# A two-layer hybrid diffusion block on one core: scratch cleared by POOL, the convolution's mean moved, and fillers and norm steps reordered on TensorE

## The chip, the cores and the metric

The kernel runs on one core of a Trainium2 chip. The metric is the device time of one execution in microseconds (us). Engines are called PE (TensorE), DVE (VectorE), ACT (ScalarE), POOL (GpSimd) and SP (SyncE, which issues the DMAs).

## The reference

256 context tokens and 256 latent tokens of width 1024 go through two layers. Cut to what matters here:

```python
for l in range(DEPTH):                      # DEPTH = 2
    mod_x, mod_c = silu(c) @ w_mod[l] + b_mod[l], silu(c_ctx) @ w_mod[l] + b_mod[l]   # 6 x 1024 each
    hx = modulate(rmsnorm(x, g_norm1[l]), mod_x[0], mod_x[1])      # hc likewise from the context
    px = split_cols(hx @ w_in[l])
    m = mlstm_mixer(...)       # matrix memory, 4 heads, both directions; then a layer norm per head
    d = diff_attention(...)    # softmax(q1 k1) - lam * softmax(q2 k2), 4 heads
    c = conv_mixer(...)        # 31 taps, then layernorm over 256 channels, then silu
    x = x + mod_x[2] * (concatenate([m, d, c]) @ w_out[l])
    h = modulate(rmsnorm(x, g_norm2[l]), mod_x[3], mod_x[4])
    x = x + mod_x[5] * (swiglu(h) if l == 0 else top_2_of_8_experts(h))
return rmsnorm(x, g_final)
```

The inputs and outputs are float32.

## The kernel before, in words

Each engine runs one hand-written program, and the order of its code is the order of its instructions; semaphores tie the engines together. Activations lie feature-major (128 features by 512 tokens, KD = 8 tiles). A weight comes in 1 MB chunks through a ring of four slots, loaded by SP: the load of chunk n waits until PE has used chunk n - 4. A product in float32 is made of three passes (`product`, L535): a leading part and a rest of both factors. The leading part is a copy, on DVE (`leading_bits`, L1539, L1540) or on ACT (`lead`, L1217) with the rest on DVE (`split_rest`, L1554).

PE is kept from idling before some waits by fillers: `spin(o, n)` (L542) issues n matmuls of ones, 128x256, whose result nobody reads. The profile shows two instructions for each float32 matmul, so n fillers are 2n rows. The tables `SPIN` and `SPIN_FIRST` hold the counts.

The places that the change touches, in the order of time:

- **Opening.** PE makes eight modulation chunks (`modulation_chunk`, L557) as they land, each followed by `SPIN_FIRST[i]` fillers. After chunk `NORM_AFTER` stands `norm(0, 0)`: column sums of squares, eight matmuls of 128x1 (L596) that wait for ACT's squares and DVE's sums. One chunk later stands `norm_spread` (L607), which spreads 1/rms over the partitions. ACT takes the root in `deviation` (L1107) and copies the modulation rows in `modulation_rows` (L1134). `turn_modulation` (L584) turns the rows into columns. After the last one DVE, ACT, DVE make the first tile of h, and the first projection starts.
- **Gate rows.** `gate_rows` on DVE clears a 64x3072 piece of the scratch (L1572), and then splits the second and third weight chunk of the projection.
- **Start of attention**, once a layer. PE: the last head's sums (`memory_sums`, L716), scores(0) (L752), the convolution's mean (`conv_mean`, L814), modulation chunks, its variance (`conv_variance`, L823, which waits for ACT's squares L1310), fillers, the transposes of the heads (L741), `conv_spread` (L830), scores(1), fillers, then the attention steps. DVE: `memory_sums`, `conv_centre` (L1844), `memory_moments`, `maxima` (L1769), and so on. ACT: a modulation row (L1134), a table load, the convolution's squares.
- **The other norms.** `norm(l, which)` on PE: fillers `SPIN["squares", ...]`, sums of squares, then `modulation(1, ...)`, which puts `norm_spread` behind its first chunk (the argument `between`).
- **Router and experts.** PE: the second norm of layer 1 as above, the logits (L914), transposes (L922), eight fillers, ranks (L930 to L934), `SPIN["moe"]` fillers, the gather of the first expert's tokens (L956), then the expert loop (L989, L1009), eight trips here.

The lines that set the norm's order before:

```python
for i in batch(l, first):
    modulation_chunk(l, first, i)
    if i == first and turned and turned[0] not in MOD_ENDS:
        turn_modulation(*turned[0])
    if i == first and between:
        between()
```

## Time and profile before

| | |
|---|---|
| median of three runs | 1466.93 us (1465.52 to 1468.47) |
| the profiled execution's own time | 1464.65 us |
| its span | 1462.9 us |
| mean granted PE clock over the span | 0.973 of full speed |
| PE busy | 1395.8 us (95%) |
| DVE / ACT / POOL busy | 982.7 / 632.6 / 181.1 us |
| HBM read | 265 MB, 182 GB/s over the span |

The span runs from the first to the last instruction; the rest of the execution's time lies around it. A busy PE includes the fillers. The granted clock is given per stretch; 1.00 is 2.4 GHz and 0.50 is 1.2 GHz.

### The profile page before, as it was taken

Reading aid. Unit: us, or ns where it says so; the run is one execution under the profiler, and the core shown is the slowest. Engines: PE = TensorE matmul, PEld = TensorE weight load, DVE = VectorE, ACT = ScalarE, POOL = GpSimd, SP = SyncE. Lnnn points to the kernel's source line nnn. Section 1 sums busy time; section 2 is a strip of 40 time slices with the busy share of each in tenths; the row PEclk is TensorE's granted clock in tenths of the full one; section 3 lists DMA queues with packets and bytes.
Section 4 is the critical chain, followed back from the end, with each engine's and each line's share of the span. In section 5 each row is a group of like instructions: output and inputs, shape, how many; then the busy total and the mean of one; then the engine's idle time right before and its main releaser. Section 6 shows DMA issues by size and latency. Waiting matters only on the chain.

```text
span 1462.9 us, 20612 instructions
## 1 busy us (share of the span) xinstructions
PE 1395.8 (95%) x7756; PEld 1144.4 (78%) x7756; DVE 982.7 (67%) x1476; ACT 632.6 (43%) x997; POOL 181.1 (12%) x134
## 2 busy tenths in 40 slices
PE   7999999989999999999999999898999999999996
PEld 4778787567688888888869887687888888888885
DVE  3755876755744344354469685656898998998896
ACT  3434334652310110010035434635677777777774
POOL 0039970000000000000003960000000000000000
PEclk8999999989999999999999999998999999999998
DMA  9254443322323222222233223149977977977940
GB/s 396 103 201 173 173 173 115 124 108 87 144 91 110 87 103 99 79 109 89 112 116 144 87 87 116 58 150 426 380 289 310 346 305 302 356 291 307 355 171 29
DMA packets 30881, 267.07 MB, mean 183 GB/s; under 512 B 3424, under 2 KB 3552, under 8 KB 4960
## 3 DMA queue, kind: packets, MB, share of 16 engines
q1 hardware_dynamic: 30816, 266.16, 47.7%
q8 instruction: 46, 0.75, 0.2%
q14 instruction: 19, 0.16, 0.0%
HBM read 265.09 MB, written 1.05 MB: 182 GB/s over the span
## 4 chain that ended last, share of the span: by engine, by line
PE 84%; DVE 8%; issue 3%; ACT 3%; DMA 2%; SPq 0%; DVEq 0%; ACTq 0%
PE ps L535 38%; PE ps L989 17%; PE ps L1009 7%; PE ps L852 3%; PE ps L557 3%; PE ps L716 2%; PE ps L752 1%; PE ps L681 1%; PE ps L771 1%; PE ps L542 1%; DMA sb_arena<-mod 1%; DVE sb_egu_lo L2007 1%; PE ps L584 1%; DVE sb_h_lo L1540 1%; PE ps L762 1%
## 5 line engine op out<-in xcount | busy, mean ns | idle before, releaser
L535 PE MATMUL ps<-sb_h_hi,sb_w_hi 128*128 128x512 f32 (+1 forms) x640 | 241.9, 378 | 3.0 <-DVE sb_w_lo L1540 2.7
L535 PE MATMUL ps<-sb_h_hi,sb_w_lo 128*128 128x512 f32 (+1 forms) x640 | 239.5, 374 | 0.0
L535 PE MATMUL ps<-sb_h_lo,sb_w_hi 128*128 128x512 f32 (+1 forms) x640 | 239.4, 374 | 0.0
L989 PE MATMUL ps<-sb_egu_lo,sb_h_lo 128*128 128x512 f32 (+1 forms) x384 | 145.2, 378 | 0.0
L535 PEld LDWEIGHTS ps<-sb_h_hi,sb_w_hi 128*128 128x128 f32 x640 | 121.1, 189 | 28.9 <-DVE sb_w_lo L1540 3.6
L535 PEld LDWEIGHTS ps<-sb_h_hi,sb_w_lo 128*128 128x128 f32 x640 | 121.0, 189 | 21.5
L535 PEld LDWEIGHTS ps<-sb_h_lo,sb_w_hi 128*128 128x128 f32 x640 | 121.2, 189 | 20.7
L1539 DVE CAST sb_w_hi<-sb_arena 128x2048 fp32r<-128x2048 f32 (+1 forms) x38 | 45.5, 1197 | 126.0 <-PE ps L535 114.7
L2007 DVE TENSOR_TENSOR sb_egu_lo<-sb_arena,sb_con_r 128x1024 fp32r<-128x1024 f32 x98 | 115.2, 1216 | 15.3 <-ACT sb_con_r L1360 15.1
L2018 DVE TENSOR_TENSOR sb_ew_lo<-sb_arena,sb_ew_hi 128x1024 fp32r<-128x1024 f32 x88 | 107.1, 1216 | 11.5 <-ACT sb_ew_hi L1373 11.5
L2152 POOL TENSOR_SCALAR sb_arena<-sb_arena,sb_small 128x512 f32<-128x512 f32 (+1 forms) x60 | 104.8, 1746 | 5.9
L1373 ACT ACTIVATE sb_ew_hi<-sb_arena 128x1024 fp32r<-128x1024 f32 x88 | 91.7, 1052 | 30.5 <-PE ps L1009 30.5
L1333 ACT ACTIVATE sb_arena<-ps 128x512 f32<-128x512 f32 x22 | 13.2, 599 | 202.1 <-PE ps L535 202.0
L2007 DVE TENSOR_TENSOR sb_egu_lo<-sb_arena,sb_x_r 128x1024 fp32r<-128x1024 f32 x82 | 96.4, 1216 | 0.5
L1360 ACT ACTIVATE sb_con_r<-sb_arena 128x1024 fp32r<-128x1024 f32 x96 | 95.9, 1051 | 0.0
L1554 DVE TENSOR_TENSOR sb_w_lo<-sb_arena,sb_w_hi 128x2048 fp32r<-128x2048 f32 x24 | 57.4, 2394 | 53.6 <-ACT sb_w_hi L1217 53.4
L989 PE MATMUL ps<-sb_con_r,sb_h_lo 128*128 128x512 f32 (+1 forms) x224 | 83.1, 371 | 3.4 <-DVE sb_egu_lo L2007 3.4
L1540 DVE TENSOR_TENSOR sb_w_lo<-sb_arena,sb_w_hi 128x2048 fp32r<-128x2048 f32 (+1 forms) x38 | 85.0, 2236 | 1.3
L989 PEld LDWEIGHTS ps<-sb_egu_lo,sb_h_lo 128*128 128x128 f32 x384 | 73.4, 191 | 13.4
L989 PE MATMUL ps<-sb_con_r,sb_hs_lo 128*128 128x512 f32 (+1 forms) x224 | 82.4, 368 | 0.0
L1360 ACT ACTIVATE sb_x_r<-sb_arena 128x1024 fp32r<-128x1024 f32 x80 | 80.4, 1059 | 0.0
L2138 POOL MEMSET sb_arena<- 128x60 f32 x2 | 0.6, 301 | 600.1 <-ACT sb_H L1119 600.1
(325 smaller groups left out, 3037.2 us busy)
## 6 DMA issues: line engine op xcount, KB each, us to landing
sb_arena<-experts SPq DMA_DIRECT2D x90, 1536.0 KB, 8.8
sb_arena<-mod SPq DMA_DIRECT2D x48, 1024.0 KB, 4.9
sb_arena<-in SPq DMA_DIRECT2D x24, 1024.0 KB, 4.8
sb_arena<-gate SPq DMA_DIRECT2D x11, 1024.0 KB, 4.8
sb_arena<-up SPq DMA_DIRECT2D x11, 1024.0 KB, 4.7
sb_arena<-out SPq DMA_DIRECT2D x8, 1024.0 KB, 6.1
sb_arena<-down SPq DMA_DIRECT2D x8, 1024.0 KB, 4.8
sb_arena<-down SPq DMA_DIRECT2D x4, 768.0 KB, 4.1
```

What stands on the lines that cost most here:

```text
L535: ins = pe.matmul(o, left[a], right[b], start=(k == first and n == 0), stop=(k == final and n == len(PRODUCTS) - 1))
L557: ins = pe.matmul(o[g * TILE:(g + 1) * TILE, 0:CHUNK], cond[:, k, at:at + TILE], w[:, k, :], start=(i == first and q == 0), stop=(i == bat ...
L989: ins = pe.matmul(o, x[:, k, :], w[:, span, :], start=(k == 0 and n == 0), stop=(k == KD - 1 and n == 2))
L1009: ins = pe.matmul(ps[:, m, :], left[a], right[b][:, m * 512:(m + 1) * 512], start=(f == 0 and n == 0), stop=(f == ET - 1 and n == len(PROD ...
L1360: f(glead[x % 4], experts[:, t, a * HALF:(a + 1) * HALF].rearrange("p (a n) -> p a n", a=4), ACT.Copy)\
L1373: f(ew_hi[:, t % 2, :], experts[:, t, 2 * HALF:], ACT.Copy).then_inc(down_leading, 1)
L1539: settled(v.tensor_copy(hi, x), ("hi", key))
L1540: v.tensor_tensor(lo, x, hi.bitcast(F32), ALU.subtract).then_inc(*dve_done.tick(key))
L1554: v.tensor_tensor(w_lo[:, n % RING], chunk_view(chunk), w_hi[:, c % SPLIT].bitcast(F32), ALU.subtract)\
L2007: v.tensor_tensor(egu_lo[t][:, a * HALF:(a + 1) * HALF].rearrange("p (a n) -> p a n", a=4), experts[:, t, a * HALF:(a + 1) * HALF].rearran ...
L2018: v.tensor_tensor(ew_lo[t][:, :], experts[:, t, 2 * HALF:], ew_hi[:, t % 2, :].bitcast(F32), ALU.subtract).then_inc(down_split, 1)
L2152: g.tensor_scalar(p, u, w[:, j:j + 1], None, ALU.mult).then_inc(*pool_done.tick(("product", l, j)))
```

## The change

DVE no longer clears the scratch; POOL does, ahead of its four small memsets, and DVE waits for it ahead of the gate arithmetic. `conv_mean` moves on PE from behind scores(0) to ahead of it, and `conv_centre` on DVE from behind the last head's sums to ahead of them. `norm_spread` now follows the sums of squares at once, with three fillers ahead of its wait (none in the opening), and the modulation chunks follow it. In the opening the norm moves one chunk ahead, ACT's root goes ahead of the first modulation row, and fillers are redistributed. Filler counts: squares (1, 0) 2 to 7, six and five new ones ahead of the convolution's variance, moe 5 to 12.

```diff
-NORM_AFTER = 3
+NORM_AFTER = 2
...
-SPIN = {("squares", 0, 0): 0, ("squares", 0, 1): 2, ("squares", 1, 0): 2, ("squares", 1, 1): 0,
+SPIN = {("squares", 0, 0): 0, ("squares", 0, 1): 2, ("squares", 1, 0): 7, ("squares", 1, 1): 0,
...
-        "router": 8, "moe": 5}
+        ("variance", 0): 6, ("variance", 1): 5, "spread": 3, "router": 8, "moe": 12}
...
-SPIN_FIRST = (8, 1, 1, 0, 1, 5, 2, 0)
+SPIN_FIRST = (8, 2, 0, 2, 1, 4, 2, 0)
...
-            def modulation(l, first, between=None):
+            def modulation(l, first):
...
-                    if i == first and between:
-                        between()
...
-                    modulation(1, MOD_NORM[l, which], lambda: norm_spread(l, which))
+                    norm_spread(l, which)
+                    modulation(1, MOD_NORM[l, which])
...
             def norm_spread(l, which):
                 lo = low(l) if which else 0
+                o = open_bank(("nscale", l, which))
+                if l + which:
+                    spin(o, SPIN["spread"])
                 pe.wait_ge(*dve_done.at(("ndiag", l, which)))
-                o = open_bank(("nscale", l, which))
...
                 memory_sums(l, NH - 1, 1)
+                conv_mean(l)
...
                 scores(0)
-                conv_mean(l)
                 fill(l, 1)
...
             def conv_variance(l):
                 lo = low(l)
+                o = open_bank(("cvar", l))
+                spin(o, SPIN["variance", l])
                 pe.wait_ge(*act_done.at(("csq", l)))
-                o = open_bank(("cvar", l))
...
             squared(0, 0)
+            deviation(0, 0)
             modulation_rows(0, 0)
-            deviation(0, 0)
...
-                settled(v.memset(scratch[0:64, 2 * T:8 * T], 0.0), ("clear", l))
                 split(("in", l, IN_ORDER[1]))
                 split(("in", l, IN_ORDER[2]))
                 dve.wait_ge(*act_done.at(("gln", l)))
+                dve.wait_ge(*pool_done.at(("clear", l)))
...
+                conv_centre(l)
                 memory_sums(l, NH - 1, 1)
-                conv_centre(l)
...
                 pool.wait_ge(*act_done.at(("h", l, 0, KD - 1)))
+                g.memset(scratch[0:64, 2 * T:8 * T], 0.0).then_inc(*pool_done.tick(("clear", l)))
                 g.memset(upad[:, :, :, 0:PAD], 0.0)
```

PE in the opening, before (L557 is a modulation chunk, L542 fillers, L596 the sums of squares, L607 the spread, L584 a turn of modulation rows):

```order
L557 MATMUL ps<-sb_arena,sb_cond 32x256 x8
L542 MATMUL ps<-sb_con 128x256
L557 MATMUL ps<-sb_arena,sb_cond 32x256 x8
L596 MATMUL ps<-sb_con,sb_arena 128x1 x8
L557 MATMUL ps<-sb_arena,sb_cond 32x256 x8
L584 MATMUL ps<-sb_con,sb_tiny 128x4x2 x2
L542 MATMUL ps<-sb_con 128x256
L607 MATMUL ps<-sb_rstd,sb_con 128x512
L557 MATMUL ps<-sb_arena,sb_cond 32x256 x8
```

and the same place now (line numbers move a little: L594 is the sums, L608 the spread, L582 the turn):

```order
L557 MATMUL ps<-sb_arena,sb_cond 32x256 x8
L594 MATMUL ps<-sb_con,sb_arena 128x1 x8
L557 MATMUL ps<-sb_arena,sb_cond 32x256 x8
L542 MATMUL ps<-sb_con 128x256 x2
L608 MATMUL ps<-sb_rstd,sb_con 128x512
L557 MATMUL ps<-sb_arena,sb_cond 32x256 x8
L582 MATMUL ps<-sb_con,sb_tiny 128x4x2 x2
L542 MATMUL ps<-sb_con 128x256
L557 MATMUL ps<-sb_arena,sb_cond 32x256 x8
```

The sums stand ahead of the fourth chunk and the spread ahead of the fifth, each one chunk earlier.

PE at the first norm of layer 1, before (L535 is the first product of the projection):

```order
L542 MATMUL ps<-sb_con 128x256 x2
L596 MATMUL ps<-sb_con,sb_H 128x1 x8
L557 MATMUL ps<-sb_arena,sb_cond 32x256 x8
L584 MATMUL ps<-sb_con,sb_modrow_odd 128x3x2 x2
L607 MATMUL ps<-sb_rstd,sb_con 128x512
L557 MATMUL ps<-sb_arena,sb_cond 32x256 x16
L542 MATMUL ps<-sb_con 128x256 x4
L535 MATMUL ps<-sb_h_hi,sb_wg_hi 128x512
```

and now:

```order
L542 MATMUL ps<-sb_con 128x256 x7
L594 MATMUL ps<-sb_con,sb_H 128x1 x8
L542 MATMUL ps<-sb_con 128x256 x3
L608 MATMUL ps<-sb_rstd,sb_con 128x512
L557 MATMUL ps<-sb_arena,sb_cond 32x256 x8
L582 MATMUL ps<-sb_con,sb_modrow_odd 128x3x2 x2
L557 MATMUL ps<-sb_arena,sb_cond 32x256 x16
L542 MATMUL ps<-sb_con 128x256 x4
```

Three fillers have taken the place of a chunk and a turn ahead of the spread, and the chunk and the turn stand behind it.

PE at the start of attention in layer 0, before (L716 the last sums, L752 scores, L814 the mean, L823 the variance):

```order
L716 MATMUL ps<-sb_arena 128x96 x20
L752 MATMUL ps<-sb_arena 128x256 x2
L814 MATMUL ps<-sb_arena,sb_con 128x512 x2
L557 MATMUL ps<-sb_arena,sb_cond 32x256 x16
L823 MATMUL ps<-sb_con,sb_kq 128x1 x8
```

and now (L718 the sums, L815 the mean, L754 scores, L825 the variance):

```order
L718 MATMUL ps<-sb_arena 128x96 x20
L815 MATMUL ps<-sb_arena,sb_con 128x512 x2
L754 MATMUL ps<-sb_arena 128x256 x2
L557 MATMUL ps<-sb_arena,sb_cond 32x256 x16
L542 MATMUL ps<-sb_con 128x256 x6
L825 MATMUL ps<-sb_con,sb_kq 128x1 x8
```

The mean and the scores have changed places, and six fillers stand ahead of the variance.

## Rows read from the trace of the kernel before

**Rows 1.** The page's first part: busy time, share of the span, instructions.
```profile
PE 1395.8 (95%) x7756; PEld 1144.4 (78%) x7756; DVE 982.7 (67%) x1476; ACT 632.6 (43%) x997; POOL 181.1 (12%) x134
```
**Rows 2.** Windows: stretch, length, busy of PE, PEld, DVE, ACT, POOL, clock, DMA, GB/s.
```profile
23.20:33.40 10.20, 10.20 (x53) 5.91 (x53) 3.18 (x6) 2.17 (x2) 0.00 (x0) 0.50 1.02 421
...
255.30:262.10 6.80, 6.03 (x17) 3.23 (x16) 4.86 (x12) 3.29 (x10) 0.00 (x0) 0.50 0.11 43
...
746.80:753.60 6.80, 6.80 (x46) 2.98 (x42) 3.14 (x6) 1.68 (x5) 0.00 (x0) 0.50 0.39 154
903.80:910.60 6.80, 5.68 (x17) 4.90 (x18) 1.61 (x6) 4.24 (x10) 0.00 (x0) 0.50 0.58 225
976.50:993.30 16.80, 16.72 (x147) 13.90 (x146) 8.06 (x40) 8.40 (x20) 0.00 (x0) 0.90 0.68 269
```
**Rows 3.** Timeline of PE, opening: start, length, instructions, idle time before and releaser.
```profile
21.49 1.07 PE L557 MATMUL ps<-sb_arena,sb_cond 128*32 128x256 f32 x16 [2.06 <-DMA sb_arena<-mod]
22.49 2.99 PE L596 MATMUL ps<-sb_con,sb_arena 128*128 128x1 f32 x16
...
29.14 1.91 PE L607 MATMUL ps<-sb_rstd,sb_con 128*128 128x512 f32 x2
...
37.52 1.07 PE L557 MATMUL ps<-sb_arena,sb_cond 128*32 128x256 f32 x16
39.10 0.61 PE L584 MATMUL ps<-sb_con,sb_modrow_odd 128*128 128x8 f32 x4 [0.50 <-ACT sb_modrow_odd L1134]
```
**Rows 4.** Timeline of PE: sums of squares, and five fillers twice.
```profile
744.75 1.92 PE L596 MATMUL ps<-sb_con,sb_H 128*128 128x1 f32 x16 [2.43 <-ACT sb_H L1100]
...
906.65 4.37 PE L542 MATMUL ps<-sb_con 128*128 128x256 f32 x10
...
993.34 2.40 PE L542 MATMUL ps<-sb_con 128*128 128x256 f32 x10
```
**Rows 5.** Timeline of ACT, the first projection chunk's leading part.
```profile
30.13 1.91 ACT L1217 ACTIVATE sb_w_hi<-sb_arena 128x2048 fp32r<-128x2048 f32 x1 [4.35 <-DMA sb_arena<-in]
```
**Rows 6.** Timeline of DVE, the clear and the split behind it.
```profile
54.48 2.62 DVE L1572 MEMSET sb_arena<- 64x3072 f32 x1 [0.58 <-issue]
...
58.40 2.29 DVE L1540 TENSOR_TENSOR sb_w_lo<-sb_arena,sb_w_hi 128x2048 fp32r<-128x2048 f32 x1
```
**Rows 7.** Timeline of PE, the product that waits for that split.
```profile
60.74 0.50 PE L535 MATMUL ps<-sb_h_hi,sb_w_hi 128*128 128x512 f32 x1 [1.53 <-DVE sb_w_lo L1540]
```
**Rows 8.** Timeline of POOL, its first memset in layer 0.
```profile
50.88 0.30 POOL L2138 MEMSET sb_arena<- 128x60 f32 x1 [50.45 <-ACT sb_H L1119]
```
**Rows 9.** Timeline of PE, start of attention in layer 0.
```profile
253.16 1.95 PE L823 MATMUL ps<-sb_con,sb_kq 128*128 128x1 f32 x16 [2.96 <-ACT sb_kq L1310]
...
257.43 2.04 PE L830 MATMUL ps<-sb_rows_n,sb_con 128*128 128x512 f32 x2 [0.78 <-ACT sb_arena L1278]
...
260.56 3.16 PE L542 MATMUL ps<-sb_con 128*128 128x256 f32 x10
...
264.71 0.44 PE L762 MATMUL ps<-sb_con,sb_arena 128*128 128x128 f32 x2
```
**Rows 10.** Timeline of PE, second norm of layer 0.
```profile
374.28 1.67 PE L607 MATMUL ps<-sb_rstd,sb_con 128*128 128x512 f32 x2 [0.36 <-DVE sb_rstd L1524]
```
**Rows 11.** Timeline of PE, first norm of layer 1.
```profile
746.60 1.81 PE L557 MATMUL ps<-sb_arena,sb_cond 128*32 128x256 f32 x16
...
749.21 2.05 PE L607 MATMUL ps<-sb_rstd,sb_con 128*128 128x512 f32 x2
...
754.23 1.99 PE L542 MATMUL ps<-sb_con 128*128 128x256 f32 x8
```
**Rows 12.** Timeline of PE, the convolution's variance in layer 1.
```profile
904.92 1.87 PE L823 MATMUL ps<-sb_con,sb_kq 128*128 128x1 f32 x8 [2.54 <-ACT sb_kq L1310]
```
**Rows 13.** Timeline of PE, the gather.
```profile
996.86 3.84 PE L956 MATMUL ps<-sb_kq,sb_H 128*128 128x128 f32 x32 [1.11 <-DVE sb_kq L1977]
```
**Rows 14.** Timeline of ACT, its first work on the gathered tokens.
```profile
1000.74 1.08 ACT L1348 ACTIVATE sb_h_lo<-ps 128x512 fp32r<-128x512 f32 x2 [12.39 <-PE ps L956]
```

## The prediction

> **What bounds the kernel now.** I read the page's busy line first. PE works 1395.8 of 1462.9 us [rows 1], so a gain must come from PE's waits, from PE's clock, or from PE work that is not needed. The timeline shows PE without a gap through the projections, the dense layer and most of the expert loop; the change touches only the seams between them. So I read the seams next, in windows with their granted clock, and then PE's timeline there. In four seams the clock stood at 0.50, which is 1.2 GHz, for 10.2, 6.8, 6.8 and 6.8 us [rows 2]. Shortly before the first fall PE had waited 2.06 us [rows 3], before the others 2.4 to 3.0 (the rows come below), and each time sums of one column stood beside the wait (L596, L823); the reader is to see that the wait itself is short and the slow stretch behind it long. The fillers show what the clock is worth: ten rows (five fillers) take 2.40 us at 993.34 and 4.37 us at 906.65 [rows 4]. So a filler costs 0.48 us at full clock and up to 0.87 at half.
>
> **The change, part by part.** Gains are negative.
>
> *A, opening.* The sums of squares took 2.99 us behind chunk 3, mostly at half clock [rows 3]; at full clock sixteen such rows take 1.92 [rows 4]. They now stand in the 2.06 us wait ahead of chunk 3. PE then holds less work than the loads need time, so the last chunk's landing is the bound. The first projection chunk was there at 30.13 [rows 5], two modulation chunks follow it in SP's order, and a chunk of 1.05 MB at 421 GB/s [rows 2] takes 2.5 us: they land near 32.6 and 35.1. The last chunk began at 37.52 [rows 3], so at most 2.4 us are gained. A new wait of some 2 us ahead of chunk 6 can drop the clock again, which would leave 1.2. I take -1.9 (0 to -2.4). ACT's exchanged root and row copy cost nothing: the row is needed only for the turn, behind the spread.
>
> *B, the clear.* DVE's memset of 2.62 us plus 0.58 us ahead of it go [rows 6]; the split behind them ended at 60.69, and PE had waited 1.53 us for it [rows 7]. PE keeps its own pace up to there, so no more than the 1.53 can be gained. POOL starts at 50.88, when the last tile of h is done [rows 8], and its memset has no row in this trace: the bounds are 0.3 us (its small ones) and several us; DVE's 2.62 [rows 6] is the nearest row. DVE needs the cleared piece only behind two splits, over 7 us of its own work (twice 3.5 us), so the wait is hidden; the pads behind it on POOL are wanted only when the convolution's input is made, much later. In layer 1 nothing is gained, as PE did not wait there. I take -1.3 (0 to -1.5). The Trainium skill's page "SBUF — State Buffer", section "Who interferes with whom", says that a DVE copy or cast in a two-port mode and a POOL instruction block each other for their whole length. By it the memset would hold DVE's cast of the last tile of h for up to 2 us, and B would be -1.1; no row here shows a POOL memset of that length.
>
> *C, attention's start in layer 0.* Moving the mean alone gains nothing: ACT's squares wait for a modulation row and a table load, not for the centred rows, and DVE only changes the order of the same work. But six fillers (2.9 us) fill the 2.96 us wait [rows 9]. With the clock up, L830 takes about 1.0 instead of 2.04, the ten filler rows 2.4 instead of 3.16 [rows 4, 9] and the scores between them 0.5 less. The 0.78 us wait of L830 [rows 9] was for the bank that the first scores held; now the mean's older bank is next in turn, which is free. Together 3.0 us until the first turn at 264.71. DVE's chain to that turn runs through the same spread and the same scores, and gains less, since its own heads' work stands between. I take -2.4 (0 to -2.9).
>
> *D, second norm of layer 0.* The spread began at 374.28 behind one chunk (1.0 us), mostly waiting for DVE [rows 10]; three fillers take 1.44. It starts 0.1 us later, and gains up to 0.7 (1.67 to 0.97) if the clock holds. The first wait and the one-column sums ahead of it are unchanged, so I doubt that: -0.1 (-0.7 to +1.5, three fillers at half clock).
>
> *E, first norm of layer 1.* Seven fillers (3.4 us) end as ACT's squares are there; two left a wait of 2.43 [rows 4]. Chunk and turn (746.60 to 749.21) leave the way of the spread. Sums until 746.67, three fillers until 748.1, spread until 749.2 at full clock; then three chunks, the turn, four fillers: 749.2 + 2.8 + 0.5 + 1.95 = 754.5, against 755.87 before (behind the fillers from 754.23 [rows 11]). The projection starts 1.4 us earlier. DVE has its first tile ready by then, since it starts 2 us earlier too. I take -1.3 (0 to -1.4).
>
> *F, attention's start in layer 1.* Five fillers fill 2.54 us [rows 12]. The ten rows at 906.65 then take 2.40 instead of about 4.2 (they end at 910.85), and the sums ahead of them about 0.95 instead of 1.87 [rows 4, 12]. DVE's normalised heads are ready when those fillers begin. I take -2.4 (0 to -2.5).
>
> *G, router.* PE is busy for 16.72 of 16.80 us between the second norm's sums and the ranks [rows 2], so what is added there moves the ranks: three fillers, 1.44, less the short wait of the spread. +1.2 (0, if the clock comes better, to +1.5).
>
> *H, fillers ahead of the experts.* Seven more fillers last 3.4 us, and PE waited only 1.11 there before the gather [rows 13]. The gather starts 2.3 us late. Behind it ACT had been idle for 12.39 us [rows 14]; it converts the tokens and then works without a gap into the loop, so the loop starts late by as much. +2.3 (0 to +3.4, if the register load between also waits for the fillers).
>
> The sum is -9.4 + 3.5 = **-5.9 us**. The profiled execution took 1464.65, its span 1462.9, and the median of the runs is 1466.93. Against the profiled execution this gives 1458.75, and on the median's scale, which I forecast, **1461.0 us**.
>
> **The rivals.**
>
> *The clock is not held (0.21).* Fillers stop the idling, but the one-column sums stay, and at 374.28 the spread took 1.67 us, so the clock fell in it, with a wait of only 0.36 us next to those sums. For it: that row [rows 10]. Against it: in E and F the empty stretch shrinks by more than half. Then A gives -1.2, B -1.3, C only the bank's 1.0, and G and H cost 3.5: 0 in all, 1466.9 us.
>
> *The expert stage does not care (0.14).* Its weights load at the same time, and if the first tiles set its start, H and part of G are free. Against it: ACT's first conversion waited for the gather, not for a load [rows 14]. Without H the time is 1458.7.
>
> *Fillers outlast their waits (0.07), the slower side.* The three fillers ahead of each spread stand on the path, and where the clock is already half when they start, they take 2.5 us each time. It decides from the point where a norm's sums begin at half clock: +1.5 in D, +2.0 in E, +2.5 in G, with H's +2.3, less A, B and the bank in C (3.5): +4.8, 1471.7 us.
>
> The change not doing what it says is excluded by the order of instructions. POOL's clear taking as much from DVE as it frees is inside B.
>
> **How the numbers follow.** The forecast's own case has 0.58. A measurement of this kernel can tell about 0.2%, 2.9 us, from no change. The forecast and the second rival are faster by more: 0.72. The first rival is within it: 0.21. Slower: 0.07. The best of all bounds is -11.4, 1455.5; I end the range there, and at the other side at 1466.0, where the forecast's case with half of its clock gains and most of the first rival's neighbourhood lie.
>
> **What would show it.** Right: the clock at 1.00 around 255, 750 and 905 on the new time axis; the last modulation chunk of the opening near 35; no wait of PE for the second split; ten filler rows of about 2.4 us ahead of layer 1's head transposes; PE busy to the very start of the gather. Wrong, for the gains: windows at 0.50 at these places again. Wrong, for the costs: a gather as early behind the ranks as the 3.5 us of before, or an expert loop that starts as early after a later gather. Wrong as a whole, if PE waits inside the projections, where it never did.

## The result, and the profile after

The changed kernel takes **1455.86 us** (median of four executions, 1453.85 to 1456.15), the kernel before 1466.22 us beside it (1465.41 to 1468.47). The ratio is 0.9924, with a 95% interval of 0.9907 to 0.9941: 10 us faster, where 5.9 were forecast. The two profiled executions differ by 8.5 us in their spans. One execution of the kernel before, of 1982.8 us at a mean granted clock of 0.648, is in a slow state and is left out everywhere below.

The first part of the changed kernel's page, against [rows 1]:

```profile
PE 1396.8 (96%) x7822; PEld 1148.8 (79%) x7822; DVE 982.6 (68%) x1474; ACT 632.5 (43%) x997; POOL 186.6 (13%) x136
```

PE has 66 instructions more and hardly more busy time, in a span 8.5 us shorter. Windows of the changed kernel at the places of [rows 2], and two that are new (columns as there):

```profile
20.90:24.30 3.40, 3.40 (x20) 1.86 (x21) 0.45 (x1) 0.38 (x1) 0.00 (x0) 0.51 1.01 422
245.00:262.00 17.00, 16.46 (x114) 10.57 (x108) 14.02 (x35) 9.26 (x23) 0.00 (x0) 1.00 0.42 146
736.00:747.00 11.00, 10.49 (x89) 7.07 (x88) 6.77 (x13) 6.42 (x12) 0.00 (x0) 1.00 0.48 174
895.00:899.00 4.00, 3.82 (x23) 3.09 (x22) 1.62 (x6) 3.02 (x8) 0.00 (x0) 1.00 0.83 328
963.20:966.60 3.40, 3.40 (x12) 2.25 (x15) 0.66 (x3) 0.07 (x1) 0.00 (x0) 0.54 0.53 217
973.50:980.30 6.80, 6.80 (x32) 6.62 (x32) 4.29 (x26) 3.07 (x9) 0.00 (x0) 0.53 1.01 416
```

The clock is up (1.00, 2.4 GHz) at both starts of attention and at the first norm of layer 1, as forecast; the opening has 3.4 us near 1.2 GHz instead of 10.2. The last two lines are the other side: the router, which had one slow stretch before, has two. PE's timeline there, from the second norm's sums to the gather:

```profile
961.95 1.02 PE L594 MATMUL ps<-sb_con,sb_arena 128*128 128x1 f32 x8 [1.12 <-ACT sb_arena L1102]
962.84 2.86 PE L542 MATMUL ps<-sb_con 128*128 128x256 f32 x6
965.49 1.00 PE L608 MATMUL ps<-sb_rstd,sb_con 128*128 128x256 f32 x2
...
970.55 4.47 PE L916 MATMUL ps<-sb_small,sb_H 128*128 128x8 f32 x32
974.88 3.65 PE L924 MATMUL ps<-sb_con,sb_H 128*128 128x128 f32 x16
...
984.06 5.43 PE L542 MATMUL ps<-sb_con 128*128 128x256 f32 x24
989.32 3.73 PE L958 MATMUL ps<-sb_kq,sb_H 128*128 128x128 f32 x32
```

Three fillers take 2.86 us, double their price at full clock, and the twelve ahead of the gather fill the wait of [rows 13] and more. The last row has no wait: the gather now stands behind its fillers.

The seams read best as distances between two fixed instructions of PE, taken from each profile's timeline. Here they are for both profiles of the kernel before (the second is experiment e5) and three of the changed one (the first, e1, e16), in us:

| stretch of PE | before | before, e5 | changed | e1 | e16 |
|---|---|---|---|---|---|
| first chunk lands | 7.49 | 6.65 | 6.68 | 6.57 | 7.24 |
| A: from there to the first product | 35.11 | 33.46 | 32.71 | 32.86 | 32.17 |
| B: first product to the second split's product | 18.14 | 18.13 | 16.63 | 16.63 | 16.63 |
| to the end of the last head's sums, layer 0 | 184.97 | 184.93 | 184.94 | 184.83 | 188.71 |
| C: from their end to the first turn | 19.00 | 18.84 | 16.05 | 16.05 | 16.05 |
| D: fillers to projection, second norm, layer 0 | 11.38 | 11.37 | 12.17 | 12.18 | 12.04 |
| E: fillers to projection, first norm, layer 1 | 14.58 | 16.21 | 13.13 | 13.19 | 13.17 |
| F: last modulation chunk to the convolution's spread | 9.98 | 10.28 | 7.21 | 7.21 | 7.21 |
| to the second norm's sums, layer 1 | 64.19 | 63.77 | 62.72 | 63.76 | 62.75 |
| G: sums to logits | 6.00 | 6.00 | 8.60 | 8.55 | 8.60 |
| logits to ranks | 10.83 | 9.17 | 12.47 | 12.49 | 12.47 |
| H: ranks to gather | 4.55 | 4.55 | 6.30 | 6.30 | 6.29 |
| gather to the output's first matmul | 452.35 | 452.02 | 451.86 | 451.82 | 452.40 |
| span | 1462.9 | 1455.9 | 1454.4 | 1456.2 | 1458.0 |

Apart from the opening (A, 0.7 us), the touched stretches repeat within 0.15 us in these three profiles of the changed kernel. Kernels of the experiments whose code at C is the same are less regular: over fourteen profiles C took 16.05 us in eight, 16.7 to 16.8 in two and 17.3 in four, while F took 7.21 in every profile with its fillers. And the kernel before alone has spans of 1462.9 and 1455.9, and the changed one 1454.4 to 1458.0: one pair of profiles doesn't carry a difference of a few microseconds.

### The profile page after: what moved, and what is told of

Read it like the earlier page. It is cut to its first block, busy times and chain, and to the rows that moved or that the text cites. A ratio compares the mean times of both kernels' runs of the same rounds, so it can differ in the third digit from the quotient of the medians.

```text
span 1454.4 us, 20738 instructions
## 1 busy us (share of the span) xinstructions
PE 1396.8 (96%) x7822; PEld 1148.8 (79%) x7822; DVE 982.6 (68%) x1474; ACT 632.5 (43%) x997; POOL 186.6 (13%) x136
## 4 chain that ended last, share of the span: by engine, by line
PE 83%; DVE 7%; ACT 4%; issue 3%; DMA 3%; SPq 0%; DVEq 0%; ACTq 0%
PE ps L535 38%; PE ps L991 17%; PE ps L1011 7%; PE ps L854 4%; PE ps L557 3%; PE ps L718 2%; DMA sb_arena<-mod 2%; PE ps L542 2%; PE ps L683 1%; PE ps L754 1%; PE ps L773 1%; DMA sb_arena<-in 1%; DVE sb_egu_lo L2009 1%; DVE sb_ew_lo L2020 1%; PE ps L582 1%
## 5 line engine op out<-in xcount | busy, mean ns | idle before, releaser
L535 PE MATMUL ps<-sb_h_hi,sb_w_hi 128*128 128x512 f32 (+1 forms) x640 | 241.8, 378 | 1.5 <-DVE sb_w_lo L1542 1.1
L535 PE MATMUL ps<-sb_h_hi,sb_w_lo 128*128 128x512 f32 (+1 forms) x640 | 239.5, 374 | 0.0
L535 PE MATMUL ps<-sb_h_lo,sb_w_hi 128*128 128x512 f32 (+1 forms) x640 | 239.4, 374 | 0.0
L535 PEld LDWEIGHTS ps<-sb_h_hi,sb_w_hi 128*128 128x128 f32 x640 | 121.1, 189 | 27.2 <-DVE sb_w_lo L1542 2.0
L535 PEld LDWEIGHTS ps<-sb_h_hi,sb_w_lo 128*128 128x128 f32 x640 | 121.0, 189 | 21.6
L535 PEld LDWEIGHTS ps<-sb_h_lo,sb_w_hi 128*128 128x128 f32 x640 | 121.1, 189 | 20.6
L2020 DVE TENSOR_TENSOR sb_ew_lo<-sb_arena,sb_ew_hi 128x1024 fp32r<-128x1024 f32 x88 | 107.2, 1218 | 11.6 <-ACT sb_ew_hi L1375 11.6
L1335 ACT ACTIVATE sb_arena<-ps 128x512 f32<-128x512 f32 x22 | 13.2, 599 | 202.1 <-PE ps L535 202.0
L2140 POOL MEMSET sb_arena<- 64x3072 f32 x2 | 5.6, 2820 | 592.0 <-ACT sb_H L1121 592.0
```

What stands on the lines that cost most here:

```text
L535: ins = pe.matmul(o, left[a], right[b], start=(k == first and n == 0), stop=(k == final and n == len(PRODUCTS) - 1))
L2020: v.tensor_tensor(ew_lo[t][:, :], experts[:, t, 2 * HALF:], ew_hi[:, t % 2, :].bitcast(F32), ALU.subtract).then_inc(down_split, 1)
```

## The experiments

Eighteen kernels ran, in five sets, each on another chip and each with executions of the kernel before beside it (e1 to e4; e5 to e8; e9 to e12; e13 to e16; e17 and e18). Ratios are against those, with 95% intervals. The median of the kernel before differs from set to set, from 1462.6 us (beside e9 to e12) to 1466.3 (beside e13 to e16), so kernels of different sets are compared by their ratios, not by their times. A difference between two experiments under some 3 us isn't shown by their medians; the stretches of the profiles can show it.

**The two kernels once more (e1, e5, e16).** No edit.

> The changed kernel once more, for the spread between its own executions. If every seam has a fixed price, the profile repeats the milestones of the first one within 0.3 us: projection at 39.4, first turn of layer 0's attention 7.7 us ahead of before, router's sums 13.5 us ahead, ranks 9.3 ahead, gather 7.5 ahead. If instead the place at which the slow stretches fall changes from execution to execution, untouched seams (attention of layer 1 past its start, which came 1.5 us closer, and router, which gave 4.2 us back) differ by a microsecond or more between the two profiles, while the touched ones stay.

> The kernel before once more, for its own spread between executions. If the costs of the seams are fixed, its profile repeats the slow stretches of rows 2 (at the first norm of layer 1, at both starts of attention) and the distances between the milestones: convolution's variance to first turn 11.55 us in layer 0, 910.85 minus 904.92 in layer 1, sums to ranks 16.8 in the router. If the place of the slow stretches is chance, one or more of these differ by 1 to 3 us, and with them what the change seemed to gain there. Ratio 1.000 in either case.

> The changed kernel a third time, in the call of these three, so that they can be held against it: 1455 to 1456 us, 9 to 10 us below before. If e13's gain and this one differ by less than 2 us, order, opening and clear are worth little in the median.

Measured: e1 1455.50 us (ratio 0.9936, 0.9915 to 0.9956), e16 1456.45 (0.9941, 0.9919 to 0.9963), e5 1464.23 (1.0006). Over all sets the kernel before has 110 executions, from 1456.7 to 1473.0, median 1464.7, mean 1464.2; the changed one 19, from 1453.9 to 1462.9, median 1455.9, mean 1456.7. Pooled like this the change is worth 7.5 us by the means and 8.8 by the medians; within its three sets, where like stands beside like, 7.7 to 11.2 by the means and 8.9 to 10.4 by the medians. The median of 1466.93 from which the forecast started lies 2.2 above that of all 110. The mean granted clock of the executions agrees: 0.983 in the changed kernel and 0.976 in the kernel before. Time at half clock is (1 - clock) / 0.5 of the span, so some 50 us against 70; rows take up to twice as long there (five fillers 4.37 us against 2.40 [rows 4]), so an estimate from these numbers is that the clock alone can be worth up to 10 us. Both theories of e1 hold in part: the touched seams repeat, untouched stretches scatter by 1 to 4 us. Windows of e5, where the kernel before had other slow stretches than in [rows 2]:

```profile
251.80:258.60 6.80, 6.29 (x22) 3.76 (x22) 4.01 (x8) 2.57 (x6) 0.00 (x0) 0.50 0.27 110
743.40:753.60 10.20, 10.20 (x63) 5.21 (x63) 4.80 (x9) 3.71 (x10) 0.00 (x0) 0.50 0.38 125
900.40:907.20 6.80, 6.33 (x19) 5.33 (x20) 1.62 (x6) 3.60 (x8) 0.00 (x0) 0.50 0.45 186
```

The falls behind both variances are there again: these belong to the code. The one at the first norm of layer 1 is 10.2 us long instead of 6.8, and costs 1.6 more.

**Gather and router (e2, e3, e4).**

```diff
-        ..., "router": 8, "moe": 12}
+        ..., "router": 8, "moe": 5}
```
```diff
-                if l + which:
+                if l + which == 1:
                     spin(o, SPIN["spread"])
```

The first is e2, the second e3, both together e4.

> The changed kernel with 5 fillers instead of 12 ahead of the gather. Theory of the prediction: the gather waits only for its fillers, starts at the ranks + 3.5 instead of + 5.3 us and the expert loop 1.8 us earlier: about 1.8 us faster than the change. Rival (the fillers pay for themselves by the clock): the wait of some 1.1 us ahead of the gather drops the clock in the gather or in the first products, the gain is under 0.5 us. Rival (the expert stage's loads set its start): gather earlier, but the first conversion and the products at the same distance from the end, no difference.

> The changed kernel without the three fillers ahead of the spread in the second norm of layer 1; those of the other norms stay. The profile of the change has the fillers at half clock there (2.86 us) and the logits partly so (4.47 against 3.63). If the fillers are on the path, 1.0 to 2.5 us come back (1.4 at full clock less a short wait of the spread, 2.5 at half) and the ranks come that much earlier behind the sums; if the fall of the clock is what costs, it falls anyway behind the wait of 1.1 us ahead of the sums, and only the fillers' own time comes back; if the fillers held something up, the difference is under 0.3 or negative.

> Both of the two: no fillers ahead of the router's spread, and 5 ahead of the gather. If the two prices lie one behind the other on PE's path, they add: 3 to 4 us faster than the change. If the loads of the experts' weights begin to set the start of the loop once PE is early, the sum is cut to the larger one, about 2 us.

Measured: e2 1454.25, e3 1454.90, e4 1453.95 us. Ranks to gather is 4.55 in e2 and e4 and 6.30 in e3: the seven fillers cost **1.75 us**, and the loop keeps its distance from the gather (7.22 us with five fillers and 7.11 with twelve), so nothing else sets its start. The three fillers ahead of the spread, however, are free. PE's timeline in e2 (with them) and in e3 (without):

```profile
964.59 1.02 PE L594 MATMUL ps<-sb_con,sb_arena 128*128 128x1 f32 x8 [1.12 <-ACT sb_arena L1102]
965.47 1.54 PE L542 MATMUL ps<-sb_con 128*128 128x256 f32 x6
966.85 0.59 PE L608 MATMUL ps<-sb_rstd,sb_con 128*128 128x256 f32 x2
...
971.50 3.92 PE L916 MATMUL ps<-sb_small,sb_H 128*128 128x8 f32 x32
```
```profile
966.53 1.02 PE L594 MATMUL ps<-sb_con,sb_arena 128*128 128x1 f32 x8 [1.12 <-ACT sb_arena L1102]
968.73 0.67 PE L608 MATMUL ps<-sb_rstd,sb_con 128*128 128x256 f32 x2 [1.17 <-DVE sb_rstd L1526]
...
973.46 3.63 PE L916 MATMUL ps<-sb_small,sb_H 128*128 128x8 f32 x32
```

Both need 6.9 us from the sums to the logits, against 6.0 before. What costs is the **order**: ACT and DVE need 1.2 us for the root and the rows of the spread, and where a modulation chunk used to stand in that time there are now fillers or a wait, with the chunk behind. The rest of the 4.2 us by which the router grew in the changed kernel is the clock. It isn't tied to the three fillers: e4, without them, has 8.61 from the sums to the logits too, because the fall hit its chunks. Nor does it come each time: of the eleven profiles with the new order here five have 8.5 to 8.6 (the changed kernel's three, e4, e11) and six 6.9.

**The old order in the second norms (e6), and fillers in their short waits (e12).**

```diff
+                    if which:
+                        modulation(1, MOD_NORM[l, which], lambda: norm_spread(l, which))
+                    else:
+                        norm_spread(l, which)
+                        modulation(1, MOD_NORM[l, which])
...
-        ..., "router": 8, "moe": 12}
+        ..., "router": 8, "moe": 5}
```

In these norms no fillers stand ahead of the spread. e12 adds to it:

```diff
-("squares", 0, 1): 2, ("squares", 1, 0): 7, ("squares", 1, 1): 0,
+("squares", 0, 1): 4, ("squares", 1, 0): 7, ("squares", 1, 1): 2,
```

> The changed kernel with two parts taken back: in the second norms of both layers the spread stands again behind the first modulation chunk, without fillers ahead of it, and 5 fillers stand ahead of the gather. Theory, from five profiles: with or without the three fillers, the new order makes PE wait out the short chain to the spread and then do the chunk behind it, which costs 0.5 to 0.65 us in layer 0 (9.47 to 10.1 us from the sums to the projection) and 0.9 in the router (6.0 to 6.9 from the sums to the logits) where the clock is the same; the seven fillers ahead of the gather cost 1.75. Together 3.1 to 3.3 us faster than the change. Rival: the price in the router is a matter of the clock alone (0.9 in three profiles, 4.2 in two, whatever the order), then the order gains nothing in layer 0's norm either and only 1.75 comes back.

> The kernel of the old second norms and 5 fillers ahead of the gather, with two more fillers ahead of each second norm's sums of squares (4 and 2), where PE waits 1.0 and 1.1 us. Theory (short waits beside one-column sums let the clock fall): the fillers fill the wait, cost nothing, and the router's slow stretch comes less often: from the sums to the ranks 15.2 to 16.8 us as before or less, total 0 to 2 us faster than without them. Rival (the one-column sums alone do it, whatever stands ahead): the same pattern, no difference; at worst 0.3 us slower where the fillers end behind the squares.

Measured: e6 1452.54 us (0.9929, 0.9907 to 0.9950), e12 1453.52 (0.9934, 0.9911 to 0.9958). Sums to logits is 6.07 in e6, and the router to its ranks 16.89; the norm of layer 0 is 11.51. The theory holds for the order; by the ratios (e6 0.9929, the change 0.9924 to 0.9941) the forecast gain of 3 us over the change is not shown. e12 shows nothing against e6: the same 16.89 in the router, 11.25 in layer 0.

**The fillers ahead of the variances away (e7), the mean back (e8).**

```diff
-        ("variance", 0): 6, ("variance", 1): 5,
+        ("variance", 0): 0, ("variance", 1): 0,
```
```diff
                 scores(0)
+                conv_mean(l)
...
                 memory_sums(l, NH - 1, 1)
+                conv_centre(l)
```

The second (e8) is the old order, with the two calls taken from where the change has them.

> The changed kernel without the six and five fillers ahead of the convolution's variance. Theory: PE waits 2.9 us in layer 0 and 2.5 in layer 1 for ACT's squares again, the clock stands at 0.5 behind it, and the stretch from the variance to the first turn is back at 11.0 to 11.5 us in layer 0 (8.7 with fillers), the one from the variance to the heads' transposes at 5.9 in layer 1 (3.2 with fillers): 5 us slower than the change. Rival (the new order of mean, scores and centring gained it, not the clock): at most 1 us slower. Rival (the old clock falls were chance): between 0 and 5, and another pattern in each layer.

> The changed kernel with the convolution's mean behind the first scores again on PE and its centring behind the last head's sums on DVE; the fillers stay. Theory of the prediction: the order alone gains nothing ahead of the variance, and behind it only the 0.78 us wait of the spread for its bank: layer 0's stretch from the sums' end to the first turn grows by 0 to 0.8 us, layer 1 is unchanged, total within 0.8 us of the change. Rival (the earlier centring is what lets DVE be ready): 1 us or more slower in layer 0, and PE waits for DVE where it does not now.

Measured: e7 1459.77 us (0.9975, 0.9960 to 0.9991), 4 us slower than the change and than e8 beside it; e8 1455.33 (0.9956, 0.9937 to 0.9974), no different from the change. PE at layer 1's variance in e7, and in the changed kernel:

```profile
903.11 1.84 PE L825 MATMUL ps<-sb_con,sb_kq 128*128 128x1 f32 x8 [2.63 <-ACT sb_kq L1312]
904.81 4.54 PE L542 MATMUL ps<-sb_con 128*128 128x256 f32 x10
```
```profile
893.02 2.43 PE L542 MATMUL ps<-sb_con 128*128 128x256 f32 x10
895.63 1.05 PE L825 MATMUL ps<-sb_con,sb_kq 128*128 128x1 f32 x8 [0.18 <-ACT sb_kq L1312]
896.55 2.41 PE L542 MATMUL ps<-sb_con 128*128 128x256 f32 x10
```

The wait is as long as the fillers that filled it, so 2.9 of the 3.0 us by which stretch F grew (10.22 against 7.21) lie behind the wait, in what the clock makes of the same rows. In layer 0 C is 18.38 in e7 and 16.79 in e8. In e8 the clock is up there, and the spread waits 1.39 us for ACT, where in the changed kernel it waits 0.36 for DVE:

```profile
252.91 1.10 PE L832 MATMUL ps<-sb_rows_n,sb_con 128*128 128x512 f32 x2 [1.39 <-ACT sb_arena L1280]
```

So the mean's move is worth 0.74 us in this profile, by the wait that the forecast had put down to the bank.

**Opening and clear (e9, e10, e14).** e9 is the changed kernel with the opening of before:

```diff
-NORM_AFTER = 2
+NORM_AFTER = 3
...
-SPIN_FIRST = (8, 2, 0, 2, 1, 4, 2, 0)
+SPIN_FIRST = (8, 1, 1, 0, 1, 5, 2, 0)
...
-            deviation(0, 0)
             modulation_rows(0, 0)
+            deviation(0, 0)
```

e10 has the clear on DVE again; e14 is the kernel before with these same lines the other way round:

```diff
+                settled(v.memset(scratch[0:64, 2 * T:8 * T], 0.0), ("clear", l))
...
-                dve.wait_ge(*pool_done.at(("clear", l)))
...
-                g.memset(scratch[0:64, 2 * T:8 * T], 0.0).then_inc(*pool_done.tick(("clear", l)))
```

> The changed kernel with the opening of before (sums of squares behind the fourth chunk, ACT's root behind the row copy, the old fillers). Theory of the prediction: PE is the bound of that opening, 33.5 to 35.1 us from the first chunk's landing to the projection, against 32.0 to 33.9 in the changed one's seven profiles, so it is 1 to 2.5 us slower than the change, all of it ahead of the first product. Rival (the opening's length is the loads' alone and the difference between two profiles of before, 1.7 us, is as large as the gain): no difference beyond chance in that stretch, under 0.5 us. Everything behind the first product as in the change, but for its own chance falls of the clock.

> The changed kernel with the clear back on DVE, none on POOL. Theory: the stretch from the first product to the split's product is 18.1 us again (16.6 in eight profiles with POOL's clear): 1.5 us slower, no more. DVE's cast of the last tile of h is 0.42 us again; in the change it takes 2.24, the time of POOL's memset beside it. Rival (the wait of 0.6 to 0.9 us near 100 us, behind which the clock fell in three of eight profiles with POOL's clear and which neither profile of before has, comes from the 1.5 us that PE is earlier): then it does not come here, and on average as much is lost as gained, the total is the same as the change's.

> The kernel before with the clear alone moved from DVE to POOL. Theory: the stretch from the first product to the split's product is 16.6 instead of 18.1 us, the cast of the last tile of h takes 2.2 us instead of 0.42, and the 1.5 us reach the end: 1.5 us faster. Rival (PE, now earlier, waits for DVE's gate rows near 100 us, the clock falls there, and the gain is lost): no difference in the median, and a wait of 0.4 us or more at that place.

Measured: e9 1458.88 us (0.9975, 0.9958 to 0.9992), 3 slower than the change and 4 slower than e10 and e11 beside it, its stretch A 35.11. PE in the changed kernel's opening, the last chunks and the first product:

```profile
31.83 1.07 PE L557 MATMUL ps<-sb_arena,sb_cond 128*32 128x256 f32 x16 [1.39 <-DMA sb_arena<-mod]
34.31 1.07 PE L557 MATMUL ps<-sb_arena,sb_cond 128*32 128x256 f32 x16 [0.35 <-DMA sb_arena<-mod]
...
39.39 0.47 PE L535 MATMUL ps<-sb_h_hi,sb_wg_hi 128*128 128x512 f32 x1 [0.64 <-DVE sb_h_lo L1542]
```

PE waits for both chunks, so the landings are the bound, as forecast. Over all profiles A is 34.9 with the old opening (five) and 32.8 with the new one (fifteen). That is 2.1 of e9's 3 to 4 us; the rest is not accounted for.

e10 1454.74 us (0.9946, 0.9928 to 0.9965), e14 1465.88 (0.9991, 0.9966 to 1.0016). Stretch B is 18.15 in e10 and 16.64 in e14: the profiles show the 1.5 us (1.2 in e11), and neither median can, as the two intervals are 5 and 7 us wide. The rival for e10 (a wait near 100 us that follows from PE being earlier) falls, since e10 has that wait and e13, also with DVE's clear, too. e14 has it as well, 0.92 us long, and the clock held behind it. As far as the end of layer 0's last sums the profiles keep the gain: from the first product to there the three with DVE's clear and no fall of the clock near 100 us take 203.1 to 203.9 us, the nine with POOL's clear, no fall and no fillers there 201.5 to 202.7. What B is worth at the end stays open, between nothing and its 1.5 us. DVE at the last tile of h and POOL's memset in the changed kernel, then DVE in e10:

```profile
47.46 0.42 DVE L1541 CAST sb_h_hi<-sb_H 128x512 fp32r<-128x512 f32 x1
47.92 0.69 DVE L1542 TENSOR_TENSOR sb_h_lo<-sb_H,sb_h_hi 128x512 fp32r<-128x512 f32 x1
48.53 2.24 DVE L1541 CAST sb_h_hi<-sb_H 128x512 fp32r<-128x512 f32 x1
```
```profile
47.67 2.82 POOL L2140 MEMSET sb_arena<- 64x3072 f32 x1 [47.23 <-ACT sb_H L1121]
```
```profile
48.56 0.42 DVE L1541 CAST sb_h_hi<-sb_H 128x512 fp32r<-128x512 f32 x1
51.30 2.62 DVE L1574 MEMSET sb_arena<- 64x3072 f32 x1 [0.58 <-issue]
```

The cast that starts beside the memset ends 0.28 us behind it and takes 1.82 us more; the subtraction that starts beside it takes its usual 0.69. That is what the Trainium skill's page "SBUF — State Buffer", section "Who interferes with whom", says of a copy or cast in a two-port mode, and the trace agrees. PE lost nothing by it: the split came just in time, and its product started at 56.02 with no wait on record. So B has its 1.5 us, and not the 1.1 that the forecast named for this case.

**The first norm of layer 1 in the old order (e11, e18), and the fillers alone (e13).** e11 is the changed kernel with the old order in that norm alone, without fillers ahead of its spread but with the seven ahead of its sums; e18 the same on the kernel of e15, where it then holds for every norm. The lines as e18 has them:

```diff
-                    norm_spread(l, which)
-                    modulation(1, MOD_NORM[l, which])
+                    modulation(1, MOD_NORM[l, which], lambda: norm_spread(l, which))
```

e13 is the kernel before with nothing but new counts:

```diff
-("squares", 1, 0): 2
+("squares", 1, 0): 7
...
+        ("variance", 0): 6, ("variance", 1): 5,
```

> The changed kernel with the old order in the first norm of layer 1 alone: chunk and turn ahead of the spread, no fillers of its own, but seven fillers ahead of the sums as in the change. Theory of the prediction: both parts gain, the seven fillers by the clock and the order by getting the spread 1.1 us earlier to DVE; the stretch from the first filler to the projection, 13.0 to 13.2 us in eight profiles against 14.6 and 16.2 before, becomes 13.2 to 14. Rival (order and its three fillers cost here too, as in the other two norms, because PE and not DVE is the bound): it becomes 12.2 to 12.7, half a microsecond or more less than in the change.

> The kernel before with the fillers alone: six and five ahead of the convolution's variance, seven instead of two ahead of layer 1's sums of squares. No order is changed. Theory (the clock carries the gain): layer 0's stretch from the sums' end to the first turn falls from 18.9 to 16.1 to 16.8 us, the one around the variance of layer 1 from 10.1 to 7.2, the one at layer 1's first norm from 14.6 and 16.2 to between 12 and 14; together 6 to 8 us faster than before, two thirds or more of the whole change. Rival (the new orders carry it, the fillers only fill): 2 us or less, and the clock falls behind the fillers too.

> The kernel of e15 with the old order in the first norm of layer 1 too (chunk and turn ahead of the spread, no fillers of its own, seven ahead of the sums). If PE bounds that seam and the clock holds, the stretch from the first filler to the projection is 11.1 to 11.7 us instead of 13.0 and the total 1.4 to 2 us below e17. Rival (the three fillers hold the clock, which falls behind the sums without them): the stretch is 13.3 again and the total the same as e17's, or the two cases come in turn and the median lies 0.5 to 1.5 us below.

Measured: e11 1455.00 us (0.9947, 0.9931 to 0.9963), e13 1461.11 (0.9962, 0.9942 to 0.9982), e18 1450.66 (0.9925, 0.9904 to 0.9946). Stretch E is 13.30 in e11, 11.14 in e13 and 11.59 in e18, against 13.23 on average over fourteen profiles of the new order. The spread in e11 and in e13:

```profile
741.42 2.00 PE L613 MATMUL ps<-sb_rstd,sb_con 128*128 128x512 f32 x2 [0.26 <-DVE sb_rstd L1531]
743.35 2.66 PE L557 MATMUL ps<-sb_arena,sb_cond 128*32 128x256 f32 x32
```
```profile
753.85 1.10 PE L607 MATMUL ps<-sb_rstd,sb_con 128*128 128x512 f32 x2
754.88 1.93 PE L557 MATMUL ps<-sb_arena,sb_cond 128*32 128x256 f32 x32
```

In e11 the clock had fallen, which is 1.6 us in these two rows alone. It fell in one of the three profiles with seven fillers and the old order, and in two of the fourteen with the new one (14.1 and 14.3 us, e9 and e7). Where it holds, E is 11.1 and 11.6 in the old order against 12.9 to 13.2 in the new, 1.3 to 2 us shorter, so the new one costs here as in the other norms; whether its fillers pay part of this back by a rarer fall, three profiles can't tell. e18's median lies 2.5 us below e17's beside it, a difference that medians of six don't show.

The fillers alone give 5.2 us where the whole change, in the same set (e16), gives 9.8 by the medians and 7.7 by the means: between half and two thirds. They do so though the profile of e13 is an unlucky one (1464.4 us, with 19.87 in C: six fillers don't always hold the clock, as C's 16.7 to 17.3 us in six of the fourteen profiles above show too).

**Two fillers at the gate rows (e15, e17).** On the kernel of e12; e17 is e15 again.

```diff
             def memory_columns(l):
+                o = open_bank(("cols", l))
+                spin(o, 2 * (l == 0))
                 pe.wait_ge(*dve_done.at(("rows", l)))
...
```

> The kernel of e12 with two more fillers ahead of the transposes of the gate rows in layer 0, where PE waited 0.4 to 0.9 us in seven of thirteen profiles and the clock fell behind it in three, at a cost of 3.5 us each time. Theory: the fillers (1.0 us) hold the clock; where the wait is there they cost up to 0.6, where it isn't 1.0; the rare 3.5 us go. On average no difference from e12 within the measurement (1453.5 us), and a stretch to layer 0's last sums of 185.0 to 186.0 and never of 188 or more. Rival (the fall has another cause than the wait): it still comes in some executions and the fillers cost 1 us.

> The kernel of e15 once more: 1450 us if its first set was typical, 1453 to 1454 (as e12) if the two fillers at the gate rows gain nothing and the first set was lucky. Its stretch to layer 0's last sums 185.0 to 186.0.

The place in e3, one of five profiles in which the clock fell behind this wait, and a window behind it:

```profile
100.93 0.71 PE L673 MATMUL ps<-sb_con,sb_rows_n 64*128 64x64 f32 x8 [0.74 <-DVE sb_rows_n L1609]
101.48 3.56 PE L683 MATMUL ps<-sb_arena 64*128 64x512 f32 x8
```
```profile
103.40:110.20 6.80, 6.80 (x29) 5.97 (x28) 2.09 (x3) 5.21 (x6) 6.52 (x4) 0.50 0.00 0
```

Measured: e15 1450.08 us (0.9905, 0.9876 to 0.9934), e17 1453.11 (0.9938, 0.9916 to 0.9959). The stretch to the last sums is 185.7 in e15, e17 and e18, and never 188.6 or more, as in five of the seventeen profiles without these fillers. With e18 these are the lowest medians of the study, 1450.1 to 1453.1 us, but the kernel before differs beside them too (1466.3 and 1462.9). By the ratios e15 has 0.9905, the same kernel again in e17 0.9938, and e18 0.9925, against 0.9924 to 0.9941 of the change; all intervals overlap. So a gain over the change is not shown, and e15's ratio may have been luck, as the expectation of e17 allowed for.

## Why the prediction was right in sign and wrong in size

The forecast was 1461.0 us and the result 1455.86, 5.1 less. Of this 2.3 are the **scale**: the sum, made from a profiled execution of 1464.65, was put on the median of 1466.93, which lies 2.2 above that of all executions of the kernel before. 0.3 lie between the changed kernel's profiled execution and its median. 2.6 are between the sum of -5.9 and the profiles' -8.5. Term by term, in us (the last column is the difference of the means over all profiles with and without the part, their numbers in brackets, so it has the chance falls on both sides):

| term | forecast | this pair of profiles | mean over the profiles |
|---|---|---|---|
| A opening | -1.9 | -2.4 | -2.1 (fifteen, five) |
| B clear | -1.3 | -1.5 | -1.5, not seen at the end |
| C attention, layer 0 | -2.4 | -2.95 | -2.4 (fourteen, three) |
| D second norm, layer 0 | -0.1 | +0.8 | +0.6 (eleven, nine) |
| E first norm, layer 1 | -1.3 | -1.45 | -1.9 (fourteen, three) |
| F attention, layer 1 | -2.4 | -2.8 | -3.0 (sixteen, four) |
| G router to its ranks | +1.2 | +4.2 | +2.3 (eleven, nine) |
| H gather | +2.3 | +1.75 | +1.75 |
| first landing, untouched stretches | 0 | -4.2 | not settled |
| sum | -5.9 | -8.5 | -6.3 without that row |

*A and B* went as the steps said: the last landing bounds the opening, the 1.5 us wait went whole. *C and F* rested on "the clock up" and on the wait being filled; that is what e7 undid. F was cut short at its own sum: its two parts, 4.2 to 2.4 and 1.87 to 0.95, add up to 2.7, and it took 2.4 with 2.5 as the bound. *H* is right in mechanism; the twelve fillers take 5.26 us to the gather (0.44 each), instead of the 5.8 that 0.48 each would give.

*The step that failed is the price of the order*, in D and G. In D the forecast says "It starts 0.1 us later" and follows only the spread. PE is the bound in this norm, and the chunk that no longer stands ahead of the spread still has to be made behind it. With the clock up in both, D is 10.6 us in the new order (e7, e9) and 9.85 in the old (e15): +0.8, where -0.1 was forecast. What stands between sums and spread has to be long enough to hide a chain of 1.2 us, and a chunk does that with work that must be done anyway. In G the size came near the truth, 0.9 of order against 1.2, for a wrong reason: the fillers are free, the displaced chunk isn't. In E the sum over PE's whole way was right (13.2 us from the first filler to the projection, 13.13 measured), but its reading was not: "Chunk and turn (746.60 to 749.21) leave the way of the spread" sounds as if this were a gain. E's gain came from the seven fillers (11.1 in e13), and the new order took 1.3 to 2 of it back.

*The other step that failed is the clock in G.* "If the clock comes better" was an end of its range, and that it could come worse was not: a wait ahead of the sums was there all the time, as PE's timeline of the kernel before shows:

```profile
975.48 1.02 PE L596 MATMUL ps<-sb_con,sb_arena 128*128 128x1 f32 x8 [1.12 <-ACT sb_arena L1100]
```

Behind it the changed kernel is at half clock in three profiles out of three, and e4 and e11 are too; six other kernels with the same order are not. The forecast's third rival had priced fillers at half clock here at +2.5, and they took 2.86 us in the changed kernel; G as a whole grew by 4.2.

*What made the result better than forecast* is none of these: D and G cost 3.9 us more than forecast, and the result was 5.1 below. On the other side stand the scale (2.3), A, B, C, E, F and H, which gained 2.4 more than forecast in this pair, and above all a term that the forecast put at nothing. It says that "the change touches only the seams between them"; yet the first landing and the untouched stretches gave 4.2 us in this pair, with the landing 0.8 earlier and attention of layer 1 1.5 shorter, in code that nobody changed. No run shows that the change did this. Together these stretches last 1333.3 us in the kernel before and 1329.1 in the changed one, but 1327.9 in e5 and 1333.4 in e16, the same two kernels again. So scatter is enough to explain it, and a forecast from one profile should have had it in its range.

Over more profiles it stays open. The sum of the terms' means, -6.3, lies near the forecast, while the executions differ by 7.5 to 11.2 us. Whether the missing 1 to 5 us are falls of the clock that became rarer elsewhere (the mean clock of 0.983 against 0.976 speaks for it) or only the sample of profiles, no run decides; e5's profile was the fastest of its ten executions. One untouched stretch does go with a touched one: from the first turn in C to the fillers of D, the eleven profiles with a C under 17 us take 103.2 to 104.0 us, the nine with a longer C 104.1 to 105.7. Why is not shown. That the forecast's range of 1455.5 to 1466.0 held the result, by 0.4 us, is luck: its lower end was the sum of all best bounds, which did not come true together.

The second rival (the expert stage does not care) falls by e2: the gather 1.75 us earlier moved the loop 1.64. The first (the clock is not held) falls by e7 and by F's 7.21 us in all sixteen profiles with its fillers; in C it is true of six profiles in fourteen, in part.

## What to carry to other kernels

Fillers paid at the three places where PE waited 2.4 to 3.0 us beside work of one column: they gave between half and two thirds of the gain, most of it behind the wait. Moving the waiting instruction forward and the useful work behind it cost 0.8 to 2 us at the three norms where PE is the bound: there, leave just enough real work between producer and consumer to hide the chain. And with a clock that falls by chance, price a seam by its stretch over several profiles, and never a change of under 1% by one pair.

## What the runs showed of the hardware

- The same program has spans of 1455.9 and 1462.9 us, and executions from 1456.7 to 1473.0. Time and mean granted clock go together, from 1456.7 us at 0.980 to 1473.0 at 0.971: slow stretches of 3.4, 6.8 or 10.2 us come at the same few seams, but not in each execution. Behind a wait of 0.6 to 0.9 us at the gate rows the clock fell in five profiles and held behind waits of 0.4 to 0.9 in five others; behind the same wait of 0.74 us the stretch to the last sums is 188.69 in e3 and 185.63 in e2, so a fall costs some 3.1 us.
- One POOL memset of 2.82 us held a DVE cast from 0.42 to 2.24 us and left a DVE subtraction at 0.69. POOL cleared 64x3072 in 2.82 us, DVE in 2.62, so POOL was 0.2 us slower.
- The first 1 MB chunk lands between 6.57 and 8.25 us, which is 1.7 us of scatter ahead of all of PE's work. Part of a late landing is made up: with 8.25 the first product of e7 starts at 40.28, with 6.67 that of e2 at 40.56.
